# Four layer norms of a float32 transformer kernel, done in two halves of the tokens

## The reference, cut to what matters

```python
for l in range(2):
    proj = h @ w_in[l]                      # 1024 -> 2818 columns, in 22 padded tiles of 128
    mixed = concatenate([nsa_mixer(...), gla_mixer(...), pool_mixer(...)])   # three token mixers, 1024 wide
    h = layer_norm_2(ALPHA * h + mixed @ w_out[l], ln1_g[l], ln1_b[l])
    ff = square(relu(h @ w_up[l])) @ w_down[l]          # 1024 -> 4096 -> 1024
    h = layer_norm_2(ALPHA * h + ff, ln2_g[l], ln2_b[l])

def layer_norm_2(x, g, b):                  # over the 1024 features of each token
    mu = mean(x); var = mean(square(x - mu))
    return (x - mu) * rsqrt(var + 1e-5) * g + b
```

## Time and profile before

| | |
|---|---|
| median of 3 runs | 2451.67 us (2450.57 to 2452.4) |
| profiled execution | 2452.37 us, span of its instructions 2450.6 us |
| TensorE matmul, weight load | 96%, 78% of the span |
| VectorE, ScalarE, GpSimd | 57%, 44%, 7% |
| granted TensorE clock, mean | 0.986 |
| loads from memory | 204.90 MB, 84 GB/s over the span |

### The profile page before, as it was taken

One profiled execution on the slowest core, in us unless ns is written; L12 is line 12 of the kernel. 1 busy time (PEld: TensorE's weight loads), 2 busy tenths in 40 slices (PEclk: granted clock), 3 DMA queues, 4 the chain that ended last, 5 costly groups with the idle time before them and its releaser, 6 DMA issues.

```text
span 2450.6 us, 33040 instructions
## 1 busy us (share of the span) xinstructions
PE 2362.8 (96%) x11802; PEld 1908.6 (78%) x11802; DVE 1407.5 (57%) x2284; ACT 1086.7 (44%) x1687; POOL 169.0 (7%) x149
## 2 busy tenths in 40 slices
PE   8889999999999999999999989999989998999997
PEld 6667888887887888888777868888867776888886
DVE  6877777435775677742647764334354677532434
ACT  4554444326886444432437543223244663422322
POOL 0511000000000000000210010000013001000000
PEclk9999999999999999999999999999999999999999
DMA  4112222222121222222221112222222112222222
GB/s 172 61 58 89 100 97 94 94 102 79 52 77 52 98 99 94 94 99 100 90 71 43 52 69 94 96 101 95 95 92 83 36 44 78 86 94 95 102 96 78
DMA packets 57405, 208.32 MB, mean 85 GB/s; under 512 B 6478, under 2 KB 6880, under 8 KB 56928
## 3 DMA queue, kind: packets, MB, share of 16 engines
q1 hardware_dynamic: 56736, 204.51, 23.7%
q0 software_dynamic: 576, 2.52, 0.3%
HBM read 204.90 MB, written 2.10 MB: 84 GB/s over the span
## 4 chain that ended last, share of the span: by engine, by line
PE 71%; issue 18%; DVE 5%; ACT 2%; POOLq 2%; POOL 1%; DMA 0%; DVEq 0%; SPq 0%; ACTq 0%
PE PS L1211 13%; PE PS L1212 13%; PE PS L1213 13%; PE PS L1239 9%; PE PS L1240 9%; PE PS L1241 9%; DVE PS L1917 1%; ACT NB L640 1%; POOLq L607 1%; PE PS L1436 1%; DVE WL L1832 1%; PE PS L1424 1%; PE PS L1270 1%; POOLq L574 1%; PE PS L1320 1%
## 5 line engine op out<-in xcount | busy, mean ns | idle before, releaser
L1832 DVE TENSOR_TENSOR WL<-RAW,WH 128x1024 fp32r<-128x1024 f32 x376 | 481.3, 1280 | 426.9 <-ACT WH L635 425.6
L1211 PE MATMUL PS<-HH,WH 128*128 128x512 f32 x1792 | 707.4, 395 | 9.0 <-DVE KR L2114 4.5
L1213 PE MATMUL PS<-HH,WL 128*128 128x512 f32 x1792 | 698.7, 390 | 0.0
L1212 PE MATMUL PS<-HL,WH 128*128 128x512 f32 x1792 | 698.5, 390 | 0.0
L635 ACT ACTIVATE WH<-RAW 128x1024 fp32r<-128x1024 f32 x376 | 397.7, 1058 | 669.1 <-PE PS L1241 411.0
L1211 PEld LDWEIGHTS PS<-HH,WH 128*128 128x128 f32 x1792 | 337.1, 188 | 85.2 <-issue 6.8
L1212 PEld LDWEIGHTS PS<-HL,WH 128*128 128x128 f32 x1792 | 337.3, 188 | 71.1 <-issue 2.9
L1213 PEld LDWEIGHTS PS<-HH,WL 128*128 128x128 f32 x1792 | 336.9, 188 | 70.9
L1241 PE MATMUL PS<-MH,WL 128*128 128x512 f32 x864 | 336.1, 389 | 0.0
L1239 PE MATMUL PS<-MH,WH 128*128 128x512 f32 x864 | 336.1, 389 | 0.0
L1240 PE MATMUL PS<-ML,WH 128*128 128x512 f32 x864 | 336.1, 389 | 0.0
(11 more groups left out here) (300 smaller groups left out, 2552.3 us busy)
## 6 DMA issues: line engine op xcount, KB each, us to landing
RAW<-wstream SPq DMA_DIRECT2D x376, 512.0 KB, 3.2
X<-xt SPq DMA_DIRECT2D x4, 512.0 KB, 7.6
W<-cmp_w POOLq DMA_DIRECT2D x2, 1024.0 KB, 5.6
out<-X SPq DMA_DIRECT2D x8, 256.0 KB, 2.0
TAB<-tables SPq DMA_DIRECT2D x1, 1871.5 KB, 13.3
WS<-spatial_w SPq DMA_DIRECT2D x1, 512.0 KB, 8.8
BS<-spatial_b SPq DMA_DIRECT2D x1, 256.0 KB, 9.3
PW<-pool_w POOLq DMA_DIRECT2D x2, 128.0 KB, 2.3
```

What stands on the lines that cost most here:

```text
L1211: pe.matmul(PS[:, bank, :], WH[:, b, w], HH[:, k, :], start=(k == 0), stop=False)
L1212: pe.matmul(PS[:, bank, :], WH[:, b, w], HL[:, k, :], start=False, stop=False)
L1213: last = pe.matmul(PS[:, bank, :], WL[:, b, w], HH[:, k, :], start=False, stop=(k == DC - 1))
L1832: dve.tensor_tensor(WL[:, b, :], RAW[:, b, :], WH[:, b, :].bitcast(F32), ALU.subtract).then_inc(w_lo, 1)
```

## The change

It cuts the 512 tokens of each of the four norms into halves of 256 (`HALVES`).

- The last output chunks come by halves: of the mixer's output chunks 4 to 7 (also in the five row slots), of the ffn's down projection chunk 7. First all first halves, then all second halves.
- Centring, squares, root, reciprocal, spreading, scaling and the parts run for one half and then for the other, at half width. The root and the reciprocal work on 64 of the 128 partitions.
- Not two but four tiles behind the norm are taken by halves (`first_half`): tiles 0 and 1 with tile 1 four k behind, tiles 2 and 3 side by side, all for the first half of the tokens, then all for the second. They use banks 0, 1, 4 and 5, and their weights need four slots at once: two more pairs of parts, `WXH` and `WXL` (`parts`, `EXTRA`).
- In TensorE's order (`seam`) the column sum of the second half stands between the first halves of tiles 0, 1 and of tiles 2, 3; its squares and spreading stand behind the latter.
- At the start of a mixer, tile 3 moves ahead of the gate logits, and `cumulate` moves behind tile 5. The compression weights `W1` are loaded after tile 3, since their place now holds `WXH` and `WXL` before that, and they have a semaphore of their own.
- The result is stored in 16 transfers of half the size.

The core of the diff:

```diff
+def half_place(name, n, h):
+    if name[:3] == "mix":
+        return 4 + 2 * h + (n - 4) // 2, n % 2
+    return (7, 4)[h], h
...
+        def parts(slot):
+            if slot in EXTRA:
+                return WXH[:, EXTRA[slot], :], WXL[:, EXTRA[slot], :]
+            return WH[:, slot % 2, :], WL[:, slot % 2, :]
...
@@ TensorE, add_rows @@
+                    if halves and n >= FIRST_HALF[halves]:
+                        for h, cols in enumerate(HALVES):
+                            to = half_out(halves, n, h)
+                            pe.matmul(to, WH[:, b, w], rh[:, cols], start=first and n % 2 == 0, stop=False)
+                            pe.matmul(to, WH[:, b, w], rl[:, cols], start=False, stop=False)
+                            last = pe.matmul(to, WL[:, b, w], rh[:, cols], start=False, stop=False)
+                        continue
...
+            def sum_half(nm, whole, h):
+                cols = HALVES[h]
+                pe.wait_ge(n_part, PART[nm, h])
+                pe.matmul(PS[:, MEAN_BANKS[h], cols], tab("ones"), MU[:, cols], start=True, stop=False)
+                pe.wait_ge(x_ready, XR[nm] + whole + (h + 1) * (DC - whole))
+                pe.matmul(PS[:, MEAN_BANKS[h], cols], tab("ones"), X[:, DC - 1, cols], start=False, stop=True).then_inc(n_add, 1)
...
+            def first_half(slot, fill, h, tiles):
+                cols = HALVES[h]
+                lag = 0 if tiles[0] else DC // 2
+                for b, k in [(b, step - b * lag) for step in range(DC + lag) for b in tiles]:
...
+                    pe.wait_ge(h_hi, fill + DC * h + k + 1)
+                    pe.matmul(PS[:, bank, cols], wh[:, w], HH[:, k, cols], start=(k == 0), stop=False)
+                    pe.matmul(PS[:, bank, cols], wl[:, w], HH[:, k, cols], start=False, stop=False)
+                    pe.wait_ge(h_lo, fill + DC * h + k + 1)
+                    last = pe.matmul(PS[:, bank, cols], wh[:, w], HL[:, k, cols], start=False, stop=(k == DC - 1))
...
+            def seam(name, nm, high, low, fill, slot):
...
+                for n in range(whole, DC):
+                    add_half(name, n, 0, high, low)
+                if whole == DC - 1:
+                    add_half(name, whole, 1, high, low, range(0, 5))
+                    sum_half(nm, whole, 0)
+                    add_half(name, whole, 1, high, low, range(5, count - 2))
+                    squares_half(nm, 0)
+                    add_half(name, whole, 1, high, low, range(count - 2, count))
+                else:
+                    add_half(name, whole, 1, high, low)
+                    sum_half(nm, whole, 0)
...
+                widen_half(nm, 0)
+                if slot is not None:
+                    first_half(slot, fill, 0, (0, 1))
+                sum_half(nm, whole, 1)
+                if slot is not None:
+                    first_half(slot, fill, 0, (2, 3))
+                squares_half(nm, 1)
+                widen_half(nm, 1)
+                if slot is not None:
+                    first_half(slot, fill, 1, (0, 1))
+                    first_half(slot, fill, 1, (2, 3))
...
@@ TensorE, start of a mixer @@
-                first_tiles(z0 // 2, H_FILL[f"in{l}"], 2)
-                tile(2)
+                if l == 0:
+                    first_tiles(z0 // 2, H_FILL["in0"], 2)
+                    project(0, z0 + 2, z_bank(2))
+                    project(0, z0 + 3, z_bank(3))
                 gate_logits()
                 swap(0)
-                tile(3)
                 tile(4)
+                tile(5)
                 cumulate()
-                tile(5)
                 hidden()
...
@@ ScalarE, up tiles @@
+                    for i in range(0 if half else 2):
+                        for b in range(2):
+                            act.wait_ge(tile_done, up + 2 * i + b + 1)
+                            act.activation(RB[:, b, :], PS[:, FIRST_BANKS[2 * i + b], :], ACT.Relu).then_inc(q_relu, 1)
+                            if i:
+                                split_hi(up // 2 + i, b + 2)
+                            act.wait_ge(q_sq, done + 2 * i + b + 1)
+                            act.activation(MH2[:, 2 * i + b, :], SB[:, b, :], ACT.Copy).then_inc(q_hi, 1)
...
@@ VectorE, layer_norm @@
+                for n in range(whole, DC):
+                    add_half(name, n, 0, scale)
+                centre_half(0)
+                for n in range(whole, DC - 2):
+                    add_half(name, n, 1, scale)
+                invert_half(0)
+                for n in range(max(whole, DC - 2), DC):
+                    add_half(name, n, 1, scale)
+                scale_half(0)
+                if first is not None:
+                    low_part(first + 2)
+                    low_part(first + 3)
+                centre_half(1)
+                invert_half(1)
+                scale_half(1)
```

380 lines of the change are left out of this document (271 added, 109 removed).

## The result

| | before | changed |
|---|---|---|
| time, median (us) | 2451.89 (2450.57 to 2452.40) | 2483.68 (2482.33 to 2484.57) |
| ratio | | 1.0134, 95% interval 1.0119 to 1.0148 |
| profiled span (us), mean granted clock of TensorE | 2450.6, 0.986 | 2482.5, 0.979 |

The change makes the kernel 1.3% slower, 31.8 us. The forecast was 2472 us with a range to 2487. So the sign and the range held, and the working came out 12 us short: it summed to 20.1. The measured time lies outside the 2464 to 2480 that the prediction calls its own range, and inside the 2480 to 2495 of its second rival, clock and pitch.

A forecast was written before the change was run, and what follows sets the result against it. TensorE, busy 96% of the span, was taken as the bound, so stops or slowing of its matmuls count. Terms 9.8 + 2.3 + 6.6 + 1.4 = 20.1 us on 2452.4 gave 2472 us; own range 2464 to 2480, wider range 2454 to 2487.

The forecast's parts named there:

- second rival: Norms: low-clock stretches cost 1 to 2 us times seven, or half matmuls take 0.13 to 0.14: 2480 to 2495 us; 17%.
- Halved matmuls at 0.12 us: TensorE's 256-wide matmuls follow each other at 0.12 us, against 0.227 for 512 columns.
- The row slots: Mixer output chunks 4 to 7 in five slots: 60 matmuls become 120 halves, +0.8 us, twice.
- Two exposed chains per norm: Each half's squares, 1.8 us, and chain from root to first high part, 3.5 us, are exposed on TensorE.
- Paced tiles 0 and 1 at 8.0 us: Behind the norm, each half of these tiles goes at 0.80 us per k, 8.0 us; matmuls alone 5.8.
- ln1: First norm of each layer, first half chunk to fifth up tile: 51.6 us against 47.5, +4.1, without the row slots.
- The fifth up tile's weights, 2.7 us: Behind the first norm, TensorE idles 2.7 us because ScalarE makes their high part only after tile 2's relu.
- ln2_0, +2.3: End of the first ffn and second norm: 50.8 us against 48.5, so +2.3 us.
- Mixers' start, +3.3 each: Tile 5's low part ends 8.7 us after the swap, with 5.4 of cover instead of 12.8: +3.3 us, twice.
- The last norm, +1.4: From chunk 7 to the span's end: 31.6 us against 30.2, +1.4; the store is no shorter.
- Rival 1: Waits before the mixers' tile 5 and the fifth up tile, 12 us together, vanish: 2460 us; 12%.
- Rival 3: Second half's chain hidden and tiles not paced, 9.7 us gone at each of three norms: 2443 us; 8%.

The follow-up runs named there:

- experiment 6: Changed kernel with the second half's sum right behind the first spreading and its squares between tiles 2 and 3 of the first half: 2477.83 us.
- experiment 9: Changed kernel with the edits of experiment 1, experiment 2, experiment 5 and experiment 6, plus the second half's spreading moved into tile 3: 2453.18 us.
- experiment 3: Changed kernel with five idle matmuls in TensorE's gaps around the spreading, for each half of each norm: 2485.09 us.
- experiment 1: Changed kernel with tile 5's low part made right behind the first turn, ahead of block additions and decay logs: 2487.47 us.
- experiment 5: Changed kernel with GpSimd's pooling windows in each mixer waiting until VectorE's sixteen block additions are done: 2483.28 us.
- experiment 7: Changed kernel with tile 5's low part ahead of the block additions and GpSimd's windows behind them: 2471.16 us.
- experiment 2: Changed kernel with the fifth and sixth up tiles' weight parts made before the relu of tile 2: 2481.48 us.
- experiment 10: Changed kernel with the edits of experiment 1, experiment 2, experiment 5 and experiment 6, plus the last norm's second-half centring and squares before first-half scaling: 2456.51 us.

## Why the prediction was right in sign and short in size

- **Halved matmuls at 0.12 us: right.** The second sum with 48 halves of tiles 2 and 3 took 6.70 us, as summed. The row slots came to 0.1 us in mixer 0, not 0.8: TensorE had a wait of 1.66 us for mixed rows among them, and 1.29 of it is left. That cover of 0.4 us was in the trace, and the term named none; the other 0.3 is open. In mixer 1 the stage is 1.4 longer, but the changed kernel has 3.4 us of half clock in it and the kernel before none there (in mixer 0 both have). The Trainium skill's gap for 256 columns ("TensorE: Matmul & The Clock Gate", "Back-to-back issue gap", 262 cycles, 0.109 us) would have made the sum 5 us smaller, by the estimate of the prediction; the timelines of the halves show one per 0.12 us, so the measurement stands.
- **Two exposed chains per norm: right**, 5.29 and 5.30 us against 1.8 + 3.5. Experiments 6 and 9 show that order is what exposes the second one: 9 and 4 us, of which the clock has some 2.5 in experiment 6.
- **Paced tiles 0 and 1 at 8.0 us: the mis-sized term.** They took 9.06 us, and the four tiles of the second half 14.7 for 13.8. Experiment 3 shows the pace at 8.06 with the clock at 1.00. The prediction knew the mechanism as its second rival, with 1 to 2 us for each of seven stretches, and gave it 17%. It was right in kind: the low clock is 1.7 us of ln1's 2.4 over the forecast. With the mixers (1.7 and 2.3) and the last norm (2.2) some 9.6 us of the changed kernel's profile are low clock for which the sum has no term, most of the 12 that it lacks. Its other half, slower halves, did not come. The range held because it took in the lower part of this rival; the working behind 2472 did not give the time. The step that failed is the sentence against it, that the gaps are shorter than before and busy stretches lie between. How much of it a run has is partly chance: in experiments 1, 5 and 7, which leave this norm's order alone, ln1 takes 52.3 to 54.5 us.
- **The fifth up tile's weights, 2.7 us: right** (2.53 and 2.54), and removable, but the total gave little of it back in experiment 2.
- **ln2_0, +2.3: right** (2.6), but with luck: the stage moves between 51.1 and 53.0 us by itself, and this profile has the 51.1.
- **Mixers' start, +3.3 each: mechanism right, size half.** 6.1 and 7.0. Of the 2.8 over in mixer 0, 0.9 is the additions beside GpSimd (experiment 5 brings them from 5.19 to 4.32 us and the wait to 3.38) and 1.7 the clock behind the wait; 0.2 is left. In mixer 1 the 3.7 over are 0.9, 2.3 for 4.6 us of tile 5 at the lower clock, and 0.5 not accounted for. The step that failed is "VectorE's order is as before": the order was, but tile 3, moved ahead of the swap, feeds GpSimd's windows sooner, and they then run beside VectorE's first additions too. The price was in the trace of before: 4.36 us for the first eight additions, with GpSimd at work for 0.3 of them, and 6.23 for the second eight, with GpSimd at work for 5.5.
- **The last norm, +1.4: 2.8.** The squares and the spreading ran at half clock, 2.2 us; the rest of the chain was shorter than summed, 0.8 us.
- **Rival 1** (weight parts in time) is out: both waits are there. **Rival 3** (faster) is out as the kernel stands; its condition, built in experiments 6 and 9, gave 13 us of TensorE's time in the norms, clock included, not the 29 it priced. That the tiles stay paced is the likely rest; no run separates it.

What stays open is why the additions fall now into 5.2 and 6.1 us and now into 6.3 or 6.4 and 8.3 with the same two engines beside each other (experiments 2, 3 and 6 show the second in mixers whose order they leave alone). GpSimd is at work for 80 to 90% of the time in both cases. Which engine gives way differs: where the additions are quick, GpSimd's next nine window instructions take 10.4 to 10.9 us in sum, where they are slow, 8.9 to 9.4.

## What to carry to other kernels

Cutting a norm in halves hides a chain only if the second half's reductions are also moved ahead of the work meant to cover them; with the halves' small sums behind that work it is exposed twice. When a step is moved, follow its output to every engine that it feeds: here a low part that was merely late could not be moved up until GpSimd, started sooner by the move, was kept off VectorE. Removing a wait in one place and finding the total unmoved is a reason to look for what the freed time ran into, and to try the two edits together: alone, 1 lost 5 us and 5 gained nothing that can be told; together they gained 10.7.

## What the hardware showed that was not expected

- **VectorE beside GpSimd.** Eight additions of 64x248 from two SBUF inputs take 4.3 us alone and 5.2 to 8.3 with GpSimd at work beside them for 80 to 90% of the time: up to nearly twice. The overlap alone does not tell which it will be, 6.10 and 8.28 us having about the same share.
- **The clock goes low behind idle time and comes back, and idle matmuls hold it.** The changed kernel spends 0.64 and 0.80 of full speed in the two paced stretches of the first norm; with five idle matmuls in the gaps of 1.45 and 1.2 us it is 1.00 in all of them. A stretch of 3.4 us at 0.50 costs 1.6 us in the ffn, where TensorE waits for nobody, and nothing in tiles that VectorE and ScalarE pace (8.04 us at 0.79). In the kernel before the same trick moves the total by 2 us, not to be told from none.
- **One stage, one program text, 51.1 to 53.0 us**, by where and how long the clock is low; a stage without edits can also carry 1.6 us of it in one run and none in another. A single profile can't price an edit below that, and the medians here can tell about 3 us.
- **Stores of 128 KB issue from one queue at 0.49 us each** in experiment 10, so sixteen of them take 7.85 us, longer than the 6.8 us from the first to the last of the sixteen half writes that they wait for.
